# A decoder layer with 32 experts: an f32 one-hot gather with a transpose behind it, a ninth weight chunk ahead, and routing inside the first block

## The reference, cut to what matters

```python
x = x + jnp.concatenate([y_s5, y_rwkv], axis=-1) @ w_out[i]
h = rms_norm(x, norm_moe_g[i])
logits = h @ router_w + router_b
top_v, top_i = lax.top_k(logits, 4)           # 4 of 32 experts for each token
gates = jax.nn.softmax(top_v, axis=-1)
# for each expert e, over its tokens xb (rows of h):
gt = jnp.minimum(xb @ w_gate[e] + b_gate[e], 7.0)
up = jnp.clip(xb @ w_up[e] + b_up[e], -7.0, 7.0)
act = (up + 1.0) * gt * jax.nn.sigmoid(1.702 * gt)
out[tokens] += gate * (act @ w_down[e] + b_down[e])
gate = jax.nn.sigmoid(rms_norm(x, norm_ple_g[i]) @ ple_w_gate[i])
x = x + (p[i] @ ple_w_proj[i]) * gate         # then a final rms_norm
```

## Time and profile before

| what | value |
|---|---|
| three runs | 1190.16, 1194.72, 1195.99 us; median 1194.72 |
| profiled execution | 1194.82 us, of which 1193.0 us are the span of the profile |
| busy share of the span | PE 90%, PE weight load 42%, DVE 30%, ACT 15%, POOL 2% |
| mean granted PE clock | 0.995 of 2.4 GHz |
| DMA | 430.42 MB, 360 GB/s read over the span |
| expert stage | from 235.5 us on; the last scatter begins at 1150.5 us |

### The profile page before, as it was taken

How to read it: one execution, slowest core, us unless ns; L and a number is a source line. 1 busy time by engine, 2 the same in 40 slices (tenths; PEclk the granted TensorE clock), 3 DMA queues, 4 the chain that set the end, 5 groups by cost and what they waited for, 6 DMA issues and landing times. The chain is left out here.

```text
span 1193.0 us, 19078 instructions
## 1 busy us (share of the span) xinstructions
PE 1079.5 (90%) x8240; PEld 499.7 (42%) x8240; DVE 360.9 (30%) x739; ACT 178.3 (15%) x297; POOL 20.8 (2%) x21
## 2 busy tenths in 40 slices
PE   8999998899999988888888888888888888888896
PEld 7788973533343333333333333333333333333342
DVE  6987826612221211111111111111212211111122
ACT  6671222400010000000000000000001000000023
POOL 0100005000000000000000000000000000000000
PEclk9999999999999999999999999999999999999999
DMA  9301193699999999999999999999999999999960
GB/s 325 128 2 45 38 363 113 269 407 428 427 429 428 428 429 429 428 428 429 430 427 428 430 429 427 428 429 430 427 429 428 430 428 428 428 430 428 428 282 35
DMA packets 44676, 430.42 MB, mean 361 GB/s; under 512 B 4960, under 2 KB 15584, under 8 KB 20064
## 3 DMA queue, kind: packets, MB, share of 16 engines
q1 hardware_dynamic: 44448, 429.37, 86.3%
q0 software_dynamic: 192, 0.52, 0.1%
HBM read 428.83 MB, written 1.05 MB: 360 GB/s over the span
## 5 line engine op out<-in xcount | busy, mean ns | idle before, releaser
L1293 PE MATMUL bank<-arena 128*64 128x512 f32 (+5 forms) x5136 | 840.7, 466 | 89.3 <-DMA arena<-in_exp_w_up 58.6
L1293 PEld LDWEIGHTS bank<-arena 128*64 128x64 f32 (+4 forms) x5136 | 305.1, 127 | 601.2 <-issue 444.4
L244 PE MATMUL bank<-arena 64*64 64x64 f32 (+8 forms) x2088 | 168.2, 265 | 9.2 <-DVE arena L869 2.9
L244 PEld LDWEIGHTS bank<-arena 64*64 64x64 f32 (+3 forms) x2088 | 135.6, 146 | 38.7 <-issue 17.8
L1485 ACT ACTIVATE arena<-arena 128x512 f32<-128x512 f32 x32 | 20.1, 630 | 519.4 <-DVE arena L1533 519.4
L1538 DVE TENSOR_SCALAR arena<-bank 128x512 f32<-128x512 f32 x32 | 22.1, 691 | 228.0 <-PE bank L1293 228.0
L1547 DVE COPY arena<-bank 128x512 f32<-128x512 f32 x32 | 22.1, 691 | 202.8 <-PE bank L1293 202.8
L1533 DVE TENSOR_SCALAR arena<-bank 128x512 f32<-128x512 f32 x32 | 22.1, 691 | 194.0 <-PE bank L1293 194.0
L1488 ACT ACTIVATE arena<-bank 128x256 f32<-128x256 f32 x32 | 12.3, 383 | 326.5 <-PE bank L1593 326.5
L1509 DVE TENSOR_TENSOR arena<-bank,par 128x512 f32<-128x512 f32 x33 | 22.8, 692 | 77.3 <-PE bank L1293 77.3
L1540 DVE SCALAR_TENSOR_TENSOR arena<-arena 128x512 f32<-128x512 f32 x32 | 33.7, 1054 | 1.1
(11 more groups left out here) (286 smaller groups left out, 423.1 us busy)
## 6 DMA issues: line engine op xcount, KB each, us to landing
arena<-in_exp_w_gate SPq DMA_DIRECT2D x64, 2048.0 KB, 32.2
arena<-in_exp_w_down SPq DMA_DIRECT2D x64, 2048.0 KB, 35.4
arena<-in_exp_w_up SPq DMA_DIRECT2D x64, 2048.0 KB, 35.3
arena<-in_w_in SPq DMA_DIRECT2D x8, 1024.0 KB, 12.3
arena<-in_w_out SPq DMA_DIRECT2D x4, 1024.0 KB, 5.6
arena<-in_ple_w_gate SPq DMA_DIRECT2D x2, 2048.0 KB, 33.5
arena<-in_xT SPq DMA_DIRECT2D x1, 1024.0 KB, 6.1
arena<-in_lora SPq DMA_DIRECT2D x1, 1024.0 KB, 13.1
```

The source lines that it names most:

```text
L244: return nc.tensor.matmul(out, lhsT, rhs, start=start, stop=stop, skip_group_check=True)
L1293: return nc.tensor.matmul(out, lhsT, rhs, start=start, stop=stop, skip_group_check=True)
```

## The change

The change has five parts.

- *Front.* xT comes in two halves with a semaphore each, the two k blocks of w_in get a semaphore each, and POOL waits for the first block before it issues the S5 loads.
- *Biases.* They are loaded earlier in SP's list, and split on DVE (`split_biases`) behind `glu_gate` of the first two scan rounds; POOL does nothing there.
- *Out-projection and routing in one block.* x is loaded earlier, into units of its own. `project_out` for the second half of the tokens is placed around the variance product, the transposes of x2 among the rest. What the second block did is now called from the first one (`route_scalar`, `route_vector`, `route_tensor`), without a block's end between.
- *Gather.* The one-hot holds the inverse norm of its token instead of 1 and is f32. x2 itself streams past it, four f32 products of 512 columns; the result has tokens on the partitions, is copied by ACT (`move_gathered`), transposed by PE between the two halves of down (`turn_gathered`), and multiplied by the gain on DVE as before. The bf16 parts are gone.
- *Chunks.* Chunks 6 and 7 (of expert 1) are issued when mix_rw is ready, 2 and 3 after the last out-projection, and a ninth chunk goes to four free units (24, 25, 26, 29) once routing is done. The first four experts are written out of the loop, since their chunks have other places. In the last block eight small products replace one PLE product, which routing now does.

The diff, cut to its core:

```diff
-        win_in = [sem("win_in_u0"), sem("win_in_u1")] + [x for n in "rkv" for x in [sem("win_in_" + n)] * 2]
+        xT_in = [sem("xT_in_low"), sem("xT_in_high")]
+        win_in = [sem("win_in_u0"), sem("win_in_u1")] + [sem("win_in_r")] * 2 + [sem("win_in_k0"), sem("win_in_k1")] + [sem("win_in_v")] * 2
...
             @block.sync
+                sp.dma_start(x_tok[:, :, :], io["x"].rearrange("(t p) d -> p t d", p=P)).then_inc(s["x_in"], 16)
+
                 sp.wait_ge(s["u0_done"], NCH)
                 sp.wait_ge(s["y_done"], NCH)
                 sp.wait_ge(s["state_done"], NCH - 1)
-                sp.dma_start(x_tok[:, :, :], io["x"].rearrange("(t p) d -> p t d", p=P)).then_inc(s["x_in"], 16)
+                sp.dma_start(slot(1), chunk_src(1, 0)).then_inc(chunk_in[1], 16)
+
+                sp.wait_ge(s["mix_rw_ready"], 2)
+                for c in (6, 7):
+                    sp.dma_start(slot(c), chunk_src(c % NC, 1)).then_inc(chunk_in[c], 16)
+                sp.wait_ge(s["out_done"], 4)
+                for c in (2, 3):
+                    sp.dma_start(slot(c), chunk_src(c, 0)).then_inc(chunk_in[c], 16)
+                sp.wait_ge(s["logits_done"], 1)
+                sp.wait_ge(s["x2_root"], 2)
+                sp.wait_ge(s["ple_done"], 4)
+                ahead = chunk_src(NSLOT % NC, 1)
+                sp.dma_start(un(24, 3), ahead[:, 0:3 * D]).then_inc(extra_in, 16)
+                sp.dma_start(un(29), ahead[:, 3 * D:4 * D]).then_inc(extra_in, 16)
...
             @block.gpsimd
+                pool.wait_ge(win_in[order[0]], 16)
...
-                pool.wait_ge(bias_in, 192)
-                pool.wait_ge(s["turned"], 6)
-                pool.wait_ge(s["bonus_ready"], 1)
...
+                    dve.wait_ge(s["head_averaged"], 4)
                     tt(mix_rw[:, :, o], yc[:, :, o], lg[:, :, o], ALU.mult).then_inc(s["mix_rw_ready"], 1)
+                def split_biases(m):
+                    dve.wait_ge(bias_in, 192)
+                    link(V.tensor_copy(bias_parts[:, m, :], bias_rest[m]))
+                    for a in (64, 96):
+                        o = slice(a, P)
+                        link(tt(bias_rest[m][o], bias_rest[m][o], bias_parts[o, m, :], ALU.subtract))
+                        last = V.tensor_copy(bias_parts[o, m, :], bias_rest[m][o])
                     if c < 2:
                         glu_gate(c)
+                        split_biases(c)
...
                 mean(1)
+                project_out(1, (0,), range(FT), True, False)
                 variance(1)
-                project_out(1, (0, 1), range(FT), True, False)
+                project_out(1, (1,), range(FT), True, False)
                 for t in range(TT):
                     pe.wait_ge(s["mix_rw_ready"], t + 1)
                     project_out(t, (0,), range(FT, KD), False, True)
+                    if t == 0:
+                        project_out(0, (1,), range(FT, KD), False, True)
+                pe.wait_ge(s["x2_ready"], 2)
+                for half in range(2):
+                    turn_x2(0, half).then_inc(s["x2_turned"], 1)
+                project_out(1, (1,), range(FT, KD - 1), False, False)
+                turn_x2(1, 0).then_inc(s["x2_turned"], 1)
+                project_out(1, (1,), range(KD - 1, KD), False, True)
+                for k in range(KD):
+                    mm(logits[0], x2T[k][:, 0:P], router[:, k, :], k == 0, k == KD - 1)
+                turn_x2(1, 1).then_inc(s["x2_turned"], 1)
+                ple_proj(2, banks[2]).then_inc(s["ple_done"], 1)
+                for k in range(KD):
+                    last = mm(logits[1], x2T[k][:, P:T], router[:, k, :], k == 0, k == KD - 1)
+                last.then_inc(s["logits_done"], 1)
+                route_tensor(pe)
...
+    def one_hot(e):
+        for t in range(TT):
+            nc.vector.tensor_scalar(onehot[:, t, :], iota[:, 0:SLOTS], rank[:, t, bass.ds(e, 1)], inv[:, t:t + 1], ALU.is_equal, ALU.mult).then_inc(s["hot_ready"], 1)
+    def gather():
+        for t in range(TT):
+            for hf in range(2):
+                last = mm(GAT[hf * 64:hf * 64 + 64, :], onehot[:, t, :], x2[:, t, hf * HF:(hf + 1) * HF], t == 0, t == TT - 1)
+        last.then_inc(s["gathered"], 1)
+    def move_gathered(act, n):
+        act.wait_ge(s["gathered"], n + 1)
+        nc.scalar.activation(by_run(xc), plain(GAT[:, :]), ACT.Copy).then_inc(s["moved"], 1)
+    def turn_gathered(pe, n):
+        pe.wait_ge(s["moved"], n + 1)
+        for k in range(4):
+            last = nc.tensor.transpose(GAT[:, k * P:(k + 1) * P], xc[:, k * P:(k + 1) * P], ident)
+        last.then_inc(s["spread"], 1)
+    def route_tensor(pe):
+        ple_proj(3, banks[3]).then_inc(mixer["ple_done"], 1)
+        ple_proj(0, banks[0]).then_inc(mixer["ple_done"], 1)
...
+        pe.wait_ge(s["hot_ready"], 2)
+        gather()
+        turn_gathered(pe, 0)
...
+        ple_proj(1, banks[1]).then_inc(mixer["ple_done"], 1)
...
+                for i in range(NSLOT + 1, QUAD * NC):
+                    sp.wait_ge(s["chunks_used"], i - NSLOT if i <= 2 * NSLOT else i - NSLOT + 1)
+                    sp.dma_start(slot((i - 1) % NSLOT), chunk_src(i % NC, i // NC)).then_inc(chunk_in[(i - 1) % NSLOT], 16)
...
                 gather()
                 pe.wait_ge(s["actT_ready"], n + 2)
                 for k in range(KD):
+                    if k == RUN:
+                        turn_gathered(pe, n + 1)
...
-            ple_proj(3, banks[7]).then_inc(t2["ple_done"], 1)
+                for _ in range(8):
+                    mm(banks[7][:, 0:P], ident, ident, True, True)
```

More of the change, by code:

```diff
@@ L179, in layer @@
         ys5 = feat(25)
[L180 to L182 removed]
+        mix_s5, mix_rw = feat(24), feat(38)
+        x_tok, x2 = (un(a, 2).rearrange("p (t d) -> p t d", d=D) for a in (26, 31))
         wout = [un(8 + 2 * c, 2).rearrange("p (k n) -> p k n", n=D) for c in range(4)]
@@ L262, in turn_x2, with ple_proj @@
             return last
+        def ple_proj(n, bank):
+            t, hf = n // 2, n % 2
+            for k in range(2):
+                last = mm(bank[:, :], pT[:, k, t * P:(t + 1) * P], wproj[:, k, hf * 512:(hf + 1) * 512], k == 0, k == 1)
+            return last
         order = [4, 5, 0, 1, 2, 3, 6, 7]
@@ L279, in slot @@
             return un(RING[c], RUN)
+        clear_expert_state, route_scalar, route_vector, route_tensor, rest = experts(nc, io, ctx, arena, con, par, banks, ring, slot, extra, sg, xc, chunk_in, extra_in, chunk_src, p_in, ple_proj, s, logits, inv, by_run, plain, x2, bias_parts, bias_down, rbias)
         with nc.Block() as block:
@@ new lines, in experts, with copy_ple, route_scalar @@
+    ple = [un(28 - n // 2)[:, (n % 2) * HF:(n % 2 + 1) * HF] for n in range(4)]
+    PLE_ORDER = (2, 3, 0, 1)
+    iota = con[:, C_IOTA:C_IOTA + P]
+    GATE, UP, GAT, YB = banks[4], banks[5], banks[6], banks[7]
+    def copy_ple(act, i):
+        act.wait_ge(mixer["ple_done"], i + 1)
+        n = PLE_ORDER[i]
+        nc.scalar.activation(ple[n], banks[n][:, :], ACT.Copy).then_inc(s["ple_copied"], 1)
+    def route_scalar(act):
+        copy_ple(act, 0)
+        act.wait_ge(s["top_ready"], 1)
+        for t in range(TT):
+            last = nc.scalar.activation(ex[:, t, 0:4], top[:, t, 0:4], ACT.Exp, bias=st[:, 2 + t:3 + t], accum_out=st[:, 4 + t:5 + t])
+        last.then_inc(s["exp_ready"], 1)
+        copy_ple(act, 1)
+        copy_ple(act, 2)
+        move_gathered(act, 0)
+        act.wait_ge(s["gates_turned"], 1)
+        nc.scalar.activation(gatesT, banks[5][:, 0:P], ACT.Copy).then_inc(s["gatesT_ready"], 1)
@@ L1434, in scatter, with open_outputs @@
+    def open_outputs(pe):
+        pe.wait_ge(s["gatesT_ready"], 1)
+        pe.wait_ge(s["ple_copied"], 4)
+        for n in range(4):
+            mm(banks[n][:, :], gatesT[rows[n], :], bias_down[rows[n], :], True, False)
     def scatter():
@@ L1614, in _ @@
-            with pe.Fori(0, n_quad) as q:
-                for place in range(QUAD):
-                    expert(q, QUAD * q + place, NC * place)
-    hT2 = un(24, 2).rearrange("p (t k c) -> p t k c", t=TT, k=KD)
-    sig = un(35, 2).rearrange("p (t d) -> p t d", d=D)
-    scr, scr2 = (un(a, 2).rearrange("p (t d) -> p t d", d=D) for a in (41, 31))
-    st2 = un(38)[:, 0:32]
-    sums, roots, inv = st2[:, 0:2], st2[:, 4:6], st2[:, 6:8]
-    sums2, roots2, inv2 = st2[:, 8:12], st2[:, 12:14], st2[:, 14:16]
@@ new lines, in _ @@
+                for place in range(QUAD):
+                    expert(None, place, NC * place)
+                with pe.Fori(1, n_quad) as q:
+                    for place in range(QUAD):
+                        expert(q, QUAD * q + place, NC * place)
+        hT2 = un(24, 2).rearrange("p (t k c) -> p t k c", t=TT, k=KD)
+        sig = un(35, 2).rearrange("p (t d) -> p t d", d=D)
+        scr, scr2 = (un(a, 2).rearrange("p (t d) -> p t d", d=D) for a in (41, 31))
+        st2 = un(38)[:, 0:32]
```

715 lines of the change are left out of this document (325 added, 390 removed).

## The result

The changed kernel takes 1187.55 us (median of 10 runs, 1186.31 to 1194.14), beside 1194.81 for the kernel before (10 runs): a ratio of 0.9945, 95% interval 0.9925 to 0.9965. In the first set of experiments it was timed again: 1188.26 beside 1194.69, 0.9942 (0.9929 to 0.9955). It is faster by 6.4 to 7.3 us, where 12.8 were forecast.

What follows compares the result with a forecast made beforehand. The prediction took the DMA weight stream in the expert stage as the bound, ended by a PE tail. Stream -11.3, front -2.3 and tail +0.8 gave -12.8: 1194.8 to 1182.0 us, own range 1178 to 1186, wide range 1176 to 1189.

Steps and rivals of the forecast that it cites:

- the cancelled gains: Whole kernel: no front gain and a slow clock together leave 1189 to 1193 us, no change; chance 0.08.
- the terms above: Spans summing to the end: mean(1) ends 184.6, to logits 29.1, to expert 0 13.1, to last up-chunk wait 894.0, then 59.4.
- the tail: After PE's last wait for an up chunk: 0.8 us longer, from the last expert's gather and turning.
- Bound: Expert stage, 390 to 1130 us: DMA's weight stream at 429 GB/s sets the pace, 29.4 us an expert; PE needs 26.0.
- a sign named for a wrong forecast: Expert stage from 400 us on: PE's waits for up and gate chunks should remain; if gone, the forecast is wrong.
- Front, -2.3: Before PE's first projection: the 2.24 us wait for w_in goes, everything later 2.3 us sooner; bounds 0 and 3.
- Bias split and out-projection, -7.2 to L: Up to the logits' end (L): mix_rw 4.6 us sooner, PE's gaps filled; logits at 216.0 instead of 223.2, before the front's gain.
- Routing, L to S in 13.1: From the logits' end (L) to expert 0's start (S): ple product ends at L + 11.0, expert 0 starts at 229.1, not 235.51.
- Stream, -11.3 in all: Weight loads: 186 chunks to come from 228.4 with 1.1 lost, instead of from 240.8; unbroken from then on, 11.3 us sooner.
- hidden but for the last expert: Expert loop: gather and turning add 0.76 us of PE per expert, 26.8 of 29.4; only the last expert's tail grows, 0.8.
- The clock, rival at 0.15: Logits to expert 0: the granted clock falls to 1.2 GHz in routing, priced at 5 us, giving 1187; chance 0.15.
- The ninth slot buys nothing, 1186.9, rival at 0.08: Before expert 0: extra chunk issued too late stands in line with refills, losing up to 4.9 us, 1186.9; chance 0.08.
- Slower by PE's bound: Expert loop: above 3.4 us more PE per expert the stream waits; at 5 us, 51 us on top, 1233; chance 0.04.

Runs made afterwards that it cites:

- the second execution: Another profiled execution of the changed kernel, without an edit: 1185.31 us.
- experiment 8: Changed kernel with the bias split back on POOL, chunks 6 and 7 waiting for it; bias loads still early: 1188.39 us, 0.9954 of the kernel before.
- the first execution: First profiled execution of the changed kernel, no edit: 1194.14 us, 6.6 above the median of its runs.
- experiment 3: Changed kernel with the extra slot loaded a second time, with chunk 17 once chunk 8 is used: 1185.29 us, 0.9909 of the kernel before.
- experiment 11: Changed kernel with each expert's gather cut to one 128-column product, only its time counting: 1184.01 us, 0.9911 of the kernel before.
- the thirteen executions: The profiled executions of the changed kernel (first and second) and of its eleven edited variants; no single time.
- experiment 2: Changed kernel without the ninth slot, its extra chunk and waits removed: 1186.99 us, 0.9938 of the kernel before.
- experiment 1: Changed kernel again without an edit, for another profile: 1188.26 us, 0.9942 of the kernel before.
- experiment 5: Changed kernel with the extra chunk in two parts, the last quarter issued first in the next block: 1185.59 us, 0.9932 of the kernel before.
- experiment 6: Changed kernel with three unused 128x128 products on PE before the block ends: 1186.77 us, 0.9944 of the kernel before.
- experiment 9: Changed kernel with the extra chunk in two parts and the extra slot loaded twice: 1181.54 us, 0.9897 of the kernel before.
- experiment 10: Changed kernel with the bias split on POOL, held until the scan's last state: 1188.13 us, 0.9946 of the kernel before.
- experiment 12: Changed kernel with the extra chunk split, its slot used twice, and five unused PE products at 50 us: 1181.49 us, 0.9897 of the kernel before.

## Why the prediction came out as it did

The direction was right; the gain was 7.3 us where 12.8 were forecast. The time lies outside the forecast's own range (1178 to 1186) and inside the wide one (1176 to 1189), whose high end was set at the edge of the cancelled gains and not for the cause that the runs show.

Of the 5.5 us missed, by the terms above, 0.7 lie in the routing, 0.4 in the tail and 3.1 in the stream, or 4.5 to 5.1 where the clock falls: 4.2 in all, or 5.6 to 6.2.

- *Bound.* Right. The stream sets the end at 29.37 us an expert in the steady stage, as before. Of the waits that were to stay, those for up chunks are there (51.3 us), those for gate chunks are gone: a sign named for a wrong forecast that came in half, since PE has less time in hand than the forecast gave it.
- *Front, -2.3.* Right within what the runs tell: 1.3 to 2.7 by time, a wait of 2.27 by the trace.
- *Bias split and out-projection, -7.2 to L.* Right by the trace: -7.5 in the second execution; no experiment took the out-projection's new order or the routing inside the first block back. Each of its parts shows: no variance gap, 0.69 and 1.12 us, no wait for mix_rw. That moving the split to DVE is what freed DVE is not shown: moved loads alone free it too (experiment 8).
- *Routing, L to S in 13.1.* 0.7 short: the ple product ends at L + 11.5 instead of 11.0, and the block's end takes 2.34 instead of 2.1.
- *Stream, -11.3 in all.* This step failed. It held that from the extra chunk on "with 1.1 lost" the rest flows unbroken, and that the gather's added PE time is "hidden but for the last expert". The measured PE time was 1.06 an expert, not 0.76; and while PE catches up it isn't hidden. The extra slot is used once, so from chunk 17 on a chunk again waits for the one eight places before it, while the stream stands one chunk further on. In the kernel before, chunk 18 was issued 47.6 us behind S (SP at 283.15), its data could flow 1.4 later, and the stream came to it at 5.3 + 10 x 4.89 = 54.2: 5.2 in hand. In the changed kernel the stream comes to it 4.9 to 5.1 sooner, and it is issued 49.9 us behind S (285.38 in the first execution), 2.3 later, with its data at 51.3, 2.2 behind the stream. So some 2 of the extra 4.9 us are given back there, and 1 at chunks 13 and 14; experiment 3 fills that hole, experiment 11 halves it in another way, and the time follows in both.
- *The clock, rival at 0.15.* It happened in part: not in the routing, but behind the block's end, in five of eight executions with the long pause. Its price was 1.7 us and not the 5 that I set. By the rule of the Trainium skill (TensorE: Matmul & The Clock Gate, section Part 1: The HAM clock gate), that half speed is the default and activity releases it, expert 0 was to begin at half speed without its warm-up products. The trace agrees in part: the granted clock was 0.50 from 226.2 to 229.2 us in the second execution, while it stayed at 1.00 behind S in eight of the thirteen executions; where it fell it cost 1.7 us, half of the 3.4 worked out by that rule.
- *The ninth slot buys nothing, 1186.9, rival at 0.08.* In outcome this is what the runs fit (experiment 2: no slower without the slot), but by another way than the one given: not a late last ple product, but 2.4 us of gain of which its own issue at the block's end, and the clock behind it where it falls, take back 1.0 to 2.7.
- *Slower by PE's bound.* No: PE's 26.36 us an expert (27.3 by its busy share, 686.97 / 740 x 29.37) stay under 29.37.

## What to carry to other kernels

Where an engine is behind a stream that waits for its buffers, its work counts in full until it has caught up, even if the steady stage has room; look at the first round trips of the ring one by one, not at the steady period. A buffer that runs ahead once is given back when the ring falls back to its old depth: use it again, or until the consumer has gained the difference. An issue placed last before a block's end is paid by all engines (1.0 us here); put it first in the next block.

## What was not expected of the hardware

A pause of 2.34 us of PE before expert 0 was followed by a granted clock of 0.83 over 225 to 235 us in the second execution, and by 1.00 in others with the same pause. The stream's pace is steadier than anything else here: 29.36 to 29.38 us an expert in the profiles of the changed kernel and of experiments 1, 3, 5, 6, 8, 9, 10 and 12.
